# The last head pair's scaling ahead of the retention output, and seven smaller moves in a five-mixer transformer kernel

## The reference

```python
def hybrid_layer(x, w_in, w_out, ...):                # run twice
    proj = x @ w_in                                   # split into 15 parts
    y_ret = retention(rq, rk, rv) * silu(rg)          # 4 heads of 64
    y_nsa = nsa(nq, ...) * silu(ng)                   # 8 heads, sparse attention, 2 branches with a softmax over tokens
    y_lru = rg_lru(lx, ...) * silu(lg)                # gated linear recurrence
    y = concatenate([y_ret, y_nsa, y_lru]) @ w_out    # 1024 x 1024
    return layer_norm(DEEPNORM_ALPHA * x + y, ln_g, ln_b)

def second_block(x, ...):
    for i in range(2):
        u = rmsnorm(h, norm_mix[i])
        h = h + (dsw_mixer, moba_mixer)[i](u, ...)    # 24 and 16 heads of 64
        h = h + square(relu(rmsnorm(h, norm_ffn[i]) @ w1)) @ w2
```

## Time and profile before

| what | value |
|---|---|
| time, median of 3 runs | 900.06 us (899.72 to 900.71) |
| the profiled execution | 900.72 us, span 898.8 us, granted clock 1.00 |
| PE, share of the span | 99%, 5614 matmuls |
| DVE, share of the span | 69% |
| ACT, share of the span | 54% |
| loads of weights, 1 MB each | 5.0 to 5.6 us from issue to landing |

### The profile page before, as it was taken

One profiled execution on the slowest core, in us unless ns is written; L12 is line 12 of the kernel. 1 busy time (PEld: TensorE's weight loads), 2 busy tenths in 40 slices (PEclk: granted clock), 3 DMA queues, 4 the chain that ended last, 5 costly groups with the idle time before them and its releaser, 6 DMA issues.

```text
span 898.8 us, 13855 instructions
## 1 busy us (share of the span) xinstructions
PE 889.1 (99%) x5614; PEld 766.7 (85%) x5614; DVE 624.4 (69%) x1084; ACT 489.7 (54%) x733; POOL 40.2 (4%) x69
## 2 busy tenths in 40 slices
PE   9999999999999999999999999999999999999998
PEld 7987878987878888877999988888877799998886
DVE  5878977879978998685766644456788486664441
ACT  7566736566737755564655543346567465554330
POOL 2600010000000000000000000000000000000000
PEclk9999999999999999999999999999999999999999
DMA  8963254633345578621655565657464266555540
GB/s 294 330 223 107 94 188 146 235 118 118 96 141 187 170 257 232 188 90 48 212 184 187 185 196 177 218 166 229 123 208 125 87 214 213 186 188 191 183 162 24
DMA packets 79455, 155.55 MB, mean 173 GB/s; under 512 B 5656, under 2 KB 7864, under 8 KB 79392
## 3 DMA queue, kind: packets, MB, share of 16 engines
q1 hardware_dynamic: 75200, 142.81, 48.4%
q0 software_dynamic: 4192, 11.85, 4.6%
HBM read 153.54 MB, written 1.11 MB: 172 GB/s over the span
## 4 chain that ended last, share of the span: by engine, by line
PE 83%; DVE 9%; ACT 4%; issue 2%; DMA 1%; SPq 0%; DVEq 0%; ACTq 0%
PE ps L764 17%; PE ps L766 16%; PE ps L765 16%; PE ps L795 8%; PE ps L797 7%; PE ps L796 7%; DVE w_lo L1896 2%; ACT w_hi L1412 1%; DMA w_raw<-in_w_in 1%; PE ps_mid L974 1%; PE ps L1065 1%; PE ps_mid L960 1%; PE ps_mid L990 1%; PE ps_mid L764 1%; ACT y_tok L1539 1%
## 5 line engine op out<-in xcount | busy, mean ns | idle before, releaser
L1896 DVE TENSOR_TENSOR w_lo<-w_raw,w_hi 128x2048 fp32r<-128x2048 f32 x133 | 299.7, 2260 | 145.1 <-ACT w_hi L1412 145.0
L1412 ACT ACTIVATE w_hi<-w_raw 128x2048 fp32r<-128x2048 f32 x133 | 250.9, 1890 | 195.6 <-PE ps L766 143.4
L764 PE MATMUL ps<-w_hi,act_hi 128*128 128x512 f32 (+1 forms) x446 | 178.0, 399 | 0.2
L766 PE MATMUL ps<-w_hi,act_lo 128*128 128x512 f32 (+1 forms) x446 | 171.1, 384 | 0.0
L765 PE MATMUL ps<-w_lo,act_hi 128*128 128x512 f32 (+1 forms) x446 | 170.7, 383 | 0.0
L764 PE MATMUL ps<-w_hi,hid 128*128 128x512 f32 x296 | 116.0, 392 | 0.0
L766 PE MATMUL ps<-w_hi,hid 128*128 128x512 f32 x296 | 115.3, 389 | 0.0
L765 PE MATMUL ps<-w_lo,hid 128*128 128x512 f32 x296 | 115.2, 389 | 0.0
L795 PE MATMUL ps<-act_hi,w_hi 128*128 128x256 f32 x384 | 110.4, 288 | 0.0
L796 PE MATMUL ps<-act_lo,w_hi 128*128 128x256 f32 x384 | 107.7, 280 | 0.0
L797 PE MATMUL ps<-act_hi,w_lo 128*128 128x256 f32 x384 | 107.4, 280 | 0.0
(11 more groups left out here) (375 smaller groups left out, 1241.0 us busy)
## 6 DMA issues: line engine op xcount, KB each, us to landing
w_raw<-in_ffn_w SPq DMA_DIRECT2D x64, 1024.0 KB, 5.4
w_raw<-in_w_in SPq DMA_DIRECT2D x21, 1024.0 KB, 5.6
w_raw<-in_a_w_qkv SPq DMA_DIRECT2D x18, 1024.0 KB, 5.1
w_raw<-in_b_w_qkv SPq DMA_DIRECT2D x12, 1024.0 KB, 5.1
w_raw<-in_w_out SPq DMA_DIRECT2D x8, 1024.0 KB, 4.9
w_raw<-in_b_w_o SPq DMA_DIRECT2D x4, 1024.0 KB, 5.0
w_raw<-in_w_in SPq DMA_DIRECT2D x12, 256.0 KB, 5.5
w_raw<-in_w_in SPq DMA_DIRECT2D x4, 512.0 KB, 3.6
```

The lines of the kernel that those rows point to most:

```text
L764: pe.matmul(o, ah, wh, start=first, stop=False)
L766: mm = pe.matmul(o, al, wh, start=False, stop=last)
L1412: act.activation(w_hi[:, c % RING, :, 0:n], w_raw[:, c % RAW, :, 0:n], ACT.Copy).then_inc(w_hi_done, 1)
L1896: dve.tensor_tensor(lo, w_raw[:, c % RAW, :, 0:n], hi.bitcast(F), ALU.subtract).then_inc(w_lo_done, 1)
```

## The change

It moves work; no operation is added or removed. In both hybrid layers: DVE does the scaling of the last pair (units 14 and 15) ahead of the retention's gating; the split of the first chunk of block o + 1 goes from hook 13 to the end of DVE's list, and stays at hook 13 on ACT with `take`, `mixed_hi` and `lru_operand` in other places; PE's `retained_acts` (L910) goes behind the transposes of unit 15; `Y_ORDER` begins with 6 and 7, and the two column blocks are no longer interleaved. In the dilated mixer a dense step goes ahead of the first scores, one `transposed` ahead of one `logits`, and a residual `take` between two parts of `acts_lo`. In the block-attention mixer the norms (hook 4) go between two `logits`, `softmax(7)` behind unit 5's staging, and one `splits` from hook 10 to hook 12.

```diff
--- before.py
+++ after.py
@@ -537,8 +537,8 @@
         BIAS_BLOCK = 0
-        Y_TILES = [0, 3, 1, 2]
-        Y_ORDER = [0, 1, 6, 7, 2, 3, 4, 5]
+        Y_TILES = [3, 0, 1, 2]
+        Y_ORDER = [6, 7, 0, 1, 2, 3, 4, 5]
@@ -1101,8 +1101,9 @@
                         ahead(1)
+                ahead(1)
                 dil_pair_scores(0)
-                ahead(8)
+                ahead(7)
                 dil_pair_scores(1)
@@ -1330,8 +1331,7 @@
                             yield from chunk_steps(b, j)
-                    yield from token_steps(o, 0, (0, 1, 6, 7))
-                    yield from token_steps(o + 1, 0, (0, 1))
+                    yield from token_steps(o, 0, (6, 7))
@@ -1346,9 +1346,9 @@
                 small = {7: lambda: lru_gates(l), 9: lambda: (nsa_pair_scores(l, 6), retention_scores(l, (0, 1))), 10: lambda: retention_scores(l, (2, 3))}
-                between = {6: lambda: compressed_transposes(l), 11: lambda: retention_output(l)}
+                between = {6: lambda: compressed_transposes(l), 11: lambda: retention_output(l), 15: lambda: retained_acts(l)}
                 late = {0: lambda: compress(l), 1: lambda: compressed_operands(l), 2: lambda: compressed_scores(l),
-                        8: lambda: retention_transposes(l), 14: lambda: retained_acts(l)}
+                        8: lambda: retention_transposes(l)}
                 scores = {0: 2, 3: 3, 5: 4, 7: 5, 11: 7}
@@ -1370,10 +1370,8 @@
                     pass
-                tokens(o, 0, (2, 3))
-                tokens(o + 1, 0, (2, 3, 6, 7))
-                for i in range(2):
-                    tokens(o + i, 0, (4, 5))
+                tokens(o, 0, (0, 1, 2, 3, 4, 5))
+                tokens(o + 1, 0, Y_ORDER)
                 pair(o, lambda: normalized_acts(l, 0), (1, 1), 1, [1])
@@ -1602,7 +1600,10 @@
                         softmax(u + 2)
-                        softmax(u + 3)
+                        if not (ph == 3 and u == 4):
+                            softmax(u + 3)
+                    if ph == 3 and u == 5:
+                        softmax(7)
                     if u in hooks:
@@ -1774,15 +1775,16 @@
                     splits(b + 4, 0)
+
+                def hook14():
                     take(b + 4, 0)
-                def hook14():
+                def hook15():
                     mixed_hi(l, 0)
-                    lru_operand(l)
...
                               6: hook6, 7: hook7, 8: hook8, 9: hook9, 10: lambda: splits(b + 3, 1), 11: hook11,
-                              13: hook13, 14: hook14}, front={4: front4, 6: front6, 8: front8})
+                              12: lambda: lru_operand(l), 13: hook13, 14: hook14, 15: hook15}, front={4: front4, 6: front6, 8: front8})
                 take(b + 4, 1)
@@ -2000,6 +2002,10 @@
                     split_lo(RING - 1)
+                elif b == FIRST["dswo"] + 1 and half == 0:
+                    acts_lo(FFN0_U, KD, 2, (0,))
+                    take(b, 0)
+                    acts_lo(FFN0_U, KD, 2, (1,))
                 elif b == FIRST["up1"] and half == 0:
@@ -2221,6 +2227,8 @@
                         logits(u + 2)
+                        if ph == 3 and u == 4:
+                            hooks[u]()
                         logits(u + 3)
@@ -2231,7 +2239,7 @@
                         staged(BLOCK_STAGED[u])
-                    if u in hooks:
+                    if u in hooks and not (ph == 3 and u == 4):
                         hooks[u]()
@@ -2304,8 +2312,8 @@
                 scaled(5)
+                transposed(3, 1)
                 logits(6)
-                transposed(3, 1)
                 logits(7)
@@ -2341,7 +2349,7 @@
-                units(3, MOBA_HEADS, {1: hook1, 2: lambda: splits(f + 3, 1), 3: lambda: splits(f + 4, 0), 4: hook4, 5: hook5, 7: lambda: splits(f + 5, 0), 10: lambda: splits(f + 5, 1), 13: lambda: splits(f + 6, 0)})
+                units(3, MOBA_HEADS, {1: hook1, 2: lambda: splits(f + 3, 1), 3: lambda: splits(f + 4, 0), 4: hook4, 5: hook5, 7: lambda: splits(f + 5, 0), 12: lambda: splits(f + 5, 1), 13: lambda: splits(f + 6, 0)})
                 pair_low(7)
@@ -2499,23 +2507,22 @@
-                def hook12():
-                    retention_norm(l)
-                    retention_gated(l)
-
                 def hook14():
                     take(b + 4, 0)
+                    lru_operand(l)
+
+                def hook15():
                     mixed_lo(l, 0)
-                    lru_operand(l)
...
                               5: hook5, 6: hook6, 7: lambda: splits(b + 2, 1), 8: hook8, 9: hook9,
-                              10: hook10, 11: hook11, 12: hook12, 13: lambda: splits(b + 4, 0), 14: hook14})
+                              10: hook10, 11: hook11, 12: lambda: retention_norm(l), 13: lambda: retention_gated(l), 14: hook14, 15: hook15})
                 gated_output(l, 0)
...
                 mixed_lo(l, 2)
+                splits(b + 4, 0)
                 splits(b + 4, 1)
@@ -2575,7 +2582,7 @@
             def lru_operand(l):
-                dve.wait_ge(at_hi, ACT0[2 * l + 1] + 2)
+                dve.wait_ge(at_hi, ACT0[2 * l + 1] + 1)
                 dve.wait_ge(lru_y, l + 1)
@@ -2656,7 +2663,7 @@
             dilated()
-            gemms("dswo", also={(1, 0): lambda: acts_lo(FFN0_U, KD, 2, (0, 1))})
+            gemms("dswo")
             gemms("up0", also={(0, 0): lambda: residual_rest(FFN0_U, 2, 1)})
...
```

## The result

The changed kernel took 907.43 us (median; 906.22 to 908.12) against 900.12 us: a ratio of 1.0076, interval 1.0063 to 1.0088. The forecast was 903.0 with a range to 905.2. So the sign was right and the size was wrong, by 4.4 us, of which the clock rival had priced 3.0.

What follows compares the result with a forecast made beforehand. It took TensorE (busy 889.1 of 898.8 us) as the bound, so only its gaps matter; +3.3 - 0.9 + 0.5 = +2.9 turned the profiled 900.72 into 903.6, or 903.0 us by the median, range 899.4 to 905.2.

Steps and rivals of the forecast that it cites:

- clock rival: Hybrid layers: the 3.1 us gap halves PE's clock for some 3 us, 1.5 us more per layer, 906; chance 0.08.
- Scaling first: Hybrid layers: DVE's scaling ends at 111.98, before PE wants it; L974's wait goes, PE 1.56 us earlier per layer.
- The walk of DVE and the new wait: Hybrid layers: last chunk ready at 125.63, PE there at 122.45; new L764 wait about 3.1 us, net +1.65 per layer.
- The loads: Hybrid layers: the weight load behind the moved split goes out at 123.4, no longer 116.3; costed at nothing.
- The clock: Hybrid layers: the granted clock stays 1.00 through the new 3.1 us gap, so no half-speed cost in the sum.
- row of 110 to 115: Profile row, 110 to 115 us: clock stayed 1.00 with a 1.41 us PE gap; taken as guide for 3.1 us.
- the row of the start-up: Profile row: L1382's same-shape matmuls last 274 to 582 ns, about two clock levels, after PE had done nothing.
- The dilated mixer: Waits at L1042, L1065 and L795 go, 1.2 with refill; 0.3 taken back for acts_lo's second half: -0.9, bounds -1.2 and 0.
- Block attention: Late softmax(7) makes PE's scores L1154 wait 1.0; moved split removes L1183's wait, 0.5: +0.5, bounds -0.7 and +1.2.
- The sum: Whole kernel: +3.3 hybrid layers, -0.9 dilated mixer, +0.5 block attention, +2.9 us in all.

Runs made afterwards that it cites:

- hybrid part alone: The kernel before with only the hybrid layers' part of the change: 906.29 us, ratio 1.0062.
- twelve fillers: The changed kernel with twelve 128x512 matmuls nobody reads on PE between the output projection's two column blocks, in each hybrid layer: 905.39 us, ratio 1.0055.
- the later parts with and without the norms' move: The kernel before with only the dilated and block-attention mixers' changes: 900.88 us, ratio 0.9999; the same without the norms' and softmax(7)'s moves: 899.36 us, ratio 0.9981.
- six fillers: The changed kernel with six matmuls nobody reads on PE between the output projection's two column blocks, in each hybrid layer: 904.30 us, ratio 1.0040.

## Why the prediction was wrong

- **Scaling first: right.** L974's wait is gone in both layers; PE was 1.33 us earlier there by the 112.32 of its timeline, and 1.56, as forecast, with the 0.23 that this execution had lost before.
- **The walk of DVE and the new wait: right.** 3.1 us forecast; 2.84 of idle time and some 0.15 of refill measured. The term was +1.65 per layer; it measured +1.77 and +1.74 wherever the clock stayed up (hybrid part alone, layer 0; fillers).
- **The loads: right.** The delayed load cost nothing in the changed kernel's trace. One execution of the twelve fillers waited for a later load (at 173.22); that the moved split had a part in it is not shown.
- **The clock: wrong, and this is the step that failed.** "I follow the row of 110 to 115, which is nearer in kind than the start, and give it 0.08." So the sum put the half-speed stretch at nothing. A gap of 1.41 us says nothing of one twice as long, and the row of the start-up spoke of what follows idle time. In place of a clock of 1.00 through the gap, the changed kernel had, by its mean clocks, lowered stretches at seven of its eight gaps, each 1.6 us. The rival's mechanism and its price (1.5 us per layer, 906) were right. That it struck so often is not explained: in the hybrid part alone gaps as long were followed by it three times in eight. The Trainium skill, "TensorE: Matmul & The Clock Gate", section "HAM oscillation — how this bites in real kernels", says that PE, when it waits for its next operand, can be throttled again and then starts at half clock. The trace agrees for layer 0: eight products at 0.43 us in place of 0.23 after 2.84 us of waiting. In layer 1 PE began again at full speed and fell 1.5 us later.
- **The dilated mixer: a size was off.** -0.9 forecast, -1.26 measured: the 0.3 taken back for the second half of acts_lo is not there.
- **Block attention: right.** +0.5 forecast, +0.55 measured; the later parts with and without the norms' move show the 1.04 of its cost. That it came out so near is in part luck: the working closes L1006's 0.2 and doesn't count it, and gives the new wait no refill, and these two nearly cancel.
- **The sum.** +3.3 (the clock left out) - 0.9 + 0.5 was +2.9; the ledger without the clock, with six fillers, has 1.74 + 1.78 - 1.26 + 0.54 = +2.80. The clock's two stretches bring it to about the changed kernel's +6.06. The median was +7.3; the 1.2 us left stay open. Two of its four executions took over 908 us, and there is no trace of them; one had a mean clock of 0.994, less than the 0.996 of two lowered stretches. The clock is the larger part of the error by far.

## What to carry to other kernels

A wait on a nearly full TensorE has two prices: its length, and, when it is long enough, a half-speed stretch that may follow it. Here that stretch cost another 1.6 us, and by the traces and mean clocks it followed ten of sixteen waits of 2.8 us, four of eight of 2.2 us and none of eight of 1.5 us. Several short gaps (0.5 to 0.7 us) cost only their length, so an operand that must come late should be asked for late, or in pieces, and not behind one long wait. When work that another engine makes is moved to the end of its queue, the consumer's order has to be read for the first use of the last piece: here it had moved from after the tenth step to after the eighth, and moving it to after the twelfth turned +0.8% into -0.1%.

## What was not expected of the hardware

Two gaps of nearly the same length in one execution (2.82 and 2.84 us) had different ends: full speed after the first, half speed from 0.8 us behind the second. Nothing that was run tells the two apart. In the changed kernel's layer 0 half speed began with the first product after the gap, at 125.95; in layer 1 PE ran at full speed for about 1.5 us from 264.6 on before it fell. Products that nobody reads kept the clock at 1.000 in eight executions of eight, with twelve and with six of them.
